# Layer norms of an encoder layer: where the low parts and the scaling by weight and bias run

## What is computed

```python
def _layer_norm(x, g, b, eps=LN_EPS):
    xf = x.astype(jnp.float32)
    mu = jnp.mean(xf, axis=-1, keepdims=True)
    var = jnp.mean(jnp.square(xf - mu), axis=-1, keepdims=True)
    return ((xf - mu) * lax.rsqrt(var + eps) * g + b).astype(x.dtype)

def layer(x, mem, l):
    x = _layer_norm(alpha * x + 0.5 * _swiglu(x, ...), ln_ffn1_g[l], ln_ffn1_b[l])
    x = _layer_norm(alpha * x + _token_mix(x, ...), ln_mix_g[l], ln_mix_b[l])
    x = _layer_norm(alpha * x + _memory_attn(x, mem, ...), ln_ca_g[l], ln_ca_b[l])
    return _layer_norm(alpha * x + 0.5 * _swiglu(x, ...), ln_ffn2_g[l], ln_ffn2_b[l])
```

## Time and profile before

| | us |
|---|---|
| median of 3 runs (4231.08 to 4235.39) | 4232.55 |
| the profiled execution, its own time | 4234.5 |
| its span in the trace | 4232.7 |
| PE busy in the span | 3664.0 (87%) |
| DVE / ACT / POOL busy | 1863.8 / 941.1 / 281.4 |
| POOL low parts (L564), 12 in ln1 to ln3, each 4.5 | 54.1 |
| stretch of ln1 (969.7 to 1037.8) | 68.1 |
| stretch of memln (2453.4 to 2489.9) | 36.5 |
| stretch of ln4 (4175 to the end) | 57.7 |

### The profile page before, as it was taken

How to read it: one execution, slowest core, us unless ns; L and a number is a source line. 1 busy time by engine, 2 the same in 40 slices (tenths; PEclk the granted TensorE clock), 3 DMA queues, 4 the chain that set the end, 5 groups by cost and what they waited for, 6 DMA issues and landing times. The chain is left out here.

```text
span 4232.7 us, 70217 instructions
## 1 busy us (share of the span) xinstructions
PE 3664.0 (87%) x29336; PEld 3110.1 (73%) x29336; DVE 1863.8 (44%) x2658; ACT 941.1 (22%) x1335; POOL 281.4 (7%) x361
## 2 busy tenths in 40 slices
PE   7999999996999545569889868977897999999997
PEld 6888888885888444248888656866785888888885
DVE  4444444446000375755444442331316454544446
ACT  2111111103111345432322332122303111111112
POOL 0000000001000052011222110010001000000000
PEclk9999999998999777779999979988998999999999
DMA  2101010101222202642122123001001010101001
GB/s 105 45 30 45 30 45 30 45 5 71 89 80 87 100 1 89 193 147 73 73 73 73 72 72 127 20 30 40 25 30 36 34 45 30 45 30 45 30 20 50
DMA packets 70899, 244.12 MB, mean 58 GB/s; under 512 B 5056, under 2 KB 30912, under 8 KB 64320
## 3 DMA queue, kind: packets, MB, share of 16 engines
q1 hardware_dynamic: 64528, 219.59, 14.6%
q10 hardware_dynamic: 6192, 21.89, 1.3%
HBM read 185.41 MB, written 56.05 MB: 57 GB/s over the span
## 5 line engine op out<-in xcount | busy, mean ns | idle before, releaser
L292 DVE TENSOR_TENSOR main_acc<-main_acc,ffn_psum 128x512 f32<-128x512 f32 (+1 forms) x1056 | 617.3, 598 | 854.2 <-PE ffn_psum L215 853.5
L204 PE MATMUL ffn_psum<-x_xh,ffn_wi_h 128*128 128x512 f32 (+1 forms) x2112 | 525.4, 357 | 52.5 <-DVE ffn_wi_l L281 52.5
L204 PE MATMUL ffn_psum<-x_xl,ffn_wi_h 128*128 128x512 f32 (+1 forms) x2112 | 525.5, 357 | 0.0
L204 PE MATMUL ffn_psum<-x_xh,ffn_wi_l 128*128 128x512 f32 (+1 forms) x2112 | 525.3, 357 | 0.0
L204 PEld LDWEIGHTS ffn_psum<-x_xh,ffn_wi_h 128*128 128x128 f32 x2112 | 372.7, 188 | 120.5 <-DVE ffn_wi_l L281 52.9
L204 PEld LDWEIGHTS ffn_psum<-x_xh,ffn_wi_l 128*128 128x128 f32 x2112 | 350.1, 188 | 60.7
L204 PEld LDWEIGHTS ffn_psum<-x_xl,ffn_wi_h 128*128 128x128 f32 x2112 | 349.7, 188 | 61.2
L215 PE MATMUL ffn_psum<-ffn_hid_h,ffn_wo_h 128*128 128x512 f32 (+1 forms) x1056 | 380.8, 361 | 12.6 <-DVE ffn_hid_l L300 10.0
L215 PE MATMUL ffn_psum<-ffn_hid_h,ffn_wo_l 128*128 128x512 f32 (+1 forms) x1056 | 377.6, 358 | 0.0
L215 PE MATMUL ffn_psum<-ffn_hid_l,ffn_wo_h 128*128 128x512 f32 (+1 forms) x1056 | 376.6, 357 | 0.0
L256 ACT CAST ffn_hid_h<-ffn_hid 128x1280 fp32r<-128x1280 f32 x44 | 55.6, 1265 | 1090.4 <-DVE ffn_hid L298 1090.4
(11 more groups left out here) (310 smaller groups left out, 5838.7 us busy)
## 6 DMA issues: line engine op xcount, KB each, us to landing
ffn_w_raw_in<-ffn_w_in_dram SPq DMA_DIRECT2D x44, 1024.0 KB, 5.3
rws_pack<-pack SPq DMA_DIRECT2D x40, 900.0 KB, 6.2
ffn_w_raw_out<-ffn_w_out_dram SPq DMA_DIRECT2D x44, 512.0 KB, 3.5
proj<-mixin_stage ACTq DMA_DIRECT2D x27, 640.0 KB, 3.0
mixin_w_raw<-mix_w_in_dram SPq DMA_DIRECT2D x27, 512.0 KB, 3.5
pack<-rwp_pack SPq DMA_DIRECT2D x4, 2580.0 KB, 10.5
rwp_raw<-proj SPq DMA_DIRECT2D x15, 640.0 KB, 8.4
kv_w_raw<-ca_w_kv_dram SPq DMA_DIRECT2D x16, 512.0 KB, 3.5
```

Source lines behind the costliest of these rows:

```text
L204: mm = nc.tensor.matmul(ps[:, at + c * BANK:at + c * BANK + tn], w[:, slot, cols], x[:, k, t0:t0 + tn], start=(k == 0 and j == 0), stop=(k ...
L292: nc.vector.tensor_tensor(acc[:, o, t0:t0 + tn], acc[:, o, t0:t0 + tn], ps[:, at:at + tn], ALU.add).then_inc(added, 1)
```

## The change

In every norm all eight tiles are scaled on ACT, and DVE scales none. The low part of every step is taken by DVE, after the normalising of the step that follows; POOL has no work in the norms. ACT's high part waits for one semaphore (`affine`) in place of two, and so does SP's store in ln4. The waiting of ACT for the constant `eps` stands at another place of the same list, before the same first instruction.

```diff
--- before.py
+++ after.py
@@ -450,9 +450,8 @@
         eps = m.sb("eps", [P, 1])
         ps = m.psum()
         mean_done, centred, squared, var_done = m.sem("mean_done"), m.sem("centred"), m.sem("squared"), m.sem("var_done")
-        rooted, rstd_done, scaled, affine_a, affine_v = m.sem("rooted"), m.sem("rstd_done"), m.sem("scaled"), m.sem("affine_a"), m.sem("affine_v")
-        high, low, const_set, stored = m.sem("high"), m.sem("low"), m.sem("const_set"), m.sem("stored")
-        HALF = KT // 2
+        const_set, rooted, rstd_done, scaled, affine = m.sem("const_set"), m.sem("rooted"), m.sem("rstd_done"), m.sem("scaled"), m.sem("affine")
+        high, low, stored = m.sem("high"), m.sem("low"), m.sem("stored")
         block = ctx.enter_context(nc.Block())
 
         def tok(s):
@@ -486,7 +485,6 @@
 
         @block.vector
         def _(dve):
-
             nc.vector.memset(eps[:], LN_EPS / scale ** 2).then_inc(const_set, 1)
 
             def centre(s):
@@ -501,15 +499,10 @@
                 dve.wait_ge(squared, s + 1)
                 nc.vector.tensor_tensor(acc[:, :, tok(s)], acc[:, :, tok(s)],
                                         rstd[:, s % 2, :].unsqueeze(1).broadcast_to([P, KT, NT]), ALU.mult).then_inc(scaled, 1)
-                dve.wait_ge(scaled, s + 1)
-                for k in range(HALF, KT):
-                    nc.vector.tensor_scalar(acc[:, k, tok(s)], acc[:, k, tok(s)], vecs[:, gain + k:gain + k + 1],
-                                            vecs[:, bias + k:bias + k + 1], ALU.mult, ALU.add).then_inc(affine_v, 1)
 
             def finish(s):
                 dve.wait_ge(high, s + 1)
-                if s == steps - 1:
-                    nc.vector.tensor_tensor(xl[:, :, tok(s)], acc[:, :, tok(s)], xh[:, :, tok(s)], ALU.subtract).then_inc(low, 1)
+                nc.vector.tensor_tensor(xl[:, :, tok(s)], acc[:, :, tok(s)], xh[:, :, tok(s)], ALU.subtract).then_inc(low, 1)
                 if after != 1.0:
                     dve.wait_ge(low, s + 1)
                     nc.vector.tensor_scalar(acc[:, :, tok(s)], acc[:, :, tok(s)], after, None, ALU.mult)
@@ -526,14 +519,13 @@
 
         @block.scalar
         def _(act):
-            act.wait_ge(const_set, 1)
-
             def square(s):
                 act.wait_ge(centred, s + 1)
                 if s >= 2:
                     act.wait_ge(var_done, s - 1)
                 nc.scalar.activation(squares[:, s % 2], acc[:, :, tok(s)], ACT.Square).then_inc(squared, 1)
 
+            act.wait_ge(const_set, 1)
             square(0)
             for s in range(steps):
                 act.wait_ge(var_done, s + 1)
@@ -543,32 +535,21 @@
                 if s + 1 < steps:
                     square(s + 1)
                 act.wait_ge(scaled, s + 1)
-                for k in range(HALF):
+                for k in range(KT):
                     nc.scalar.activation(acc[:, k, tok(s)], acc[:, k, tok(s)], ACT.Identity,
                                          bias=vecs[:, bias + k:bias + k + 1],
-                                         scale=vecs[:, gain + k:gain + k + 1]).then_inc(affine_a, 1)
+                                         scale=vecs[:, gain + k:gain + k + 1]).then_inc(affine, 1)
                 if out_d is None:
-                    act.wait_ge(affine_v, HALF * (s + 1))
-                    act.wait_ge(affine_a, HALF * (s + 1))
+                    act.wait_ge(affine, KT * (s + 1))
                     nc.scalar.copy(xh[:, :, tok(s)], acc[:, :, tok(s)]).then_inc(high, 1)
 
-        if out_d is None:
-            @block.sync
-            def _(sp):
+        @block.sync
+        def _(sp):
+            if out_d is None:
                 weights.start(sp)
-
-            @block.gpsimd
-            def _(pool):
-                for s in range(steps - 1):
-                    pool.wait_ge(high, s + 1)
-                    nc.gpsimd.tensor_tensor(xl[:, :, tok(s)], acc[:, :, tok(s)], xh[:, :, tok(s)],
-                                            ALU.subtract).then_inc(low, 1)
-        else:
-            @block.sync
-            def _(sp):
+            else:
                 for s in range(steps):
-                    sp.wait_ge(affine_a, HALF * (s + 1))
-                    sp.wait_ge(affine_v, HALF * (s + 1))
+                    sp.wait_ge(affine, KT * (s + 1))
                     sp.dma_start(out_d[:, :, tok(s)], acc[:, :, tok(s)]).then_inc(stored, 16)
                 sp.wait_ge(stored, 16 * steps)
```

## The result

| | before | after |
|---|---|---|
| median of 20 runs (lowest to highest), us | 4233.4 (4229.98 to 4241.03) | 4241.16 (4235.89 to 4248.87) |
| ratio, 95% interval | | 1.0018 (1.0011 to 1.0024) |
| span of the profiled execution | 4232.7 | 4239.6 |
| ln1: first root to end of its last instruction | 54.41 | 54.87 |
| memln, the same | 21.89 | 23.40 |

The change makes the kernel 7.8 us slower, 0.18%; forecast was 10.2 slower, 4242.8, in a range of 4239 to 4247. From their first roots on the five norms are 8.6 longer in the two traces (0.46 + 1.51 + 0.48 + 0.54 + 5.59).

The account below looks back on a forecast made before the run. The five norms were taken as bound by the chain inside each step, through ACT, with DVE limiting ln4's middle steps. +4.3 us for four norms and +5.9 for ln4 made +10.2 on 4232.55: 4242.8, range 4239 to 4247.

Parts of the forecast that it names:

- Root to scaling 4.62: In a norm step without POOL's disturbance, the time from ACT's root to the start of scaling: 4.62 us.
- the pitch of 0.493: Start-to-start spacing of ACT's scalings, 0.493 us, so four more add 1.97 in each of 22 steps.
- the 2.25 that POOL had put on the path: POOL's low part holds up DVE's normalising, some 2.25 us in each of 13 steps; the change removes it.
- the low part at 2.29 or less: Low part moved to DVE behind the next step's normalising: takes 2.29 us and costs nothing.
- the cover on DVE in ln3: In ln3 DVE finishes low part, factor and centring before ACT wants the centring, half a microsecond to spare.
- the step of 8.57 in ln4: In ln4 ACT's scaling becomes the limit: 4.62 to the scaling plus 3.95 to the next root, 8.57 us.
- Rival B: Norms: normalising is long for another reason than POOL's reading, so the stall stays, 29.3 us more, 4272; chance 0.03.
- rival A: Norms: scaling is cheaper on ACT without DVE scaling beside it, pitch 0.37, 11.4 us faster, 4221; chance 0.03.
- Rival C: DVE's cover fails in ln3, and PE's sums may slow in ln4: +1 to +4 us, 4244 to 4247; chance 0.09.
- I take nothing for it: Semaphores, one wait in place of two and one fewer to clear: counted as no change in time.
- I take 0.2: ln4: PE's last sum of squares slowed after idle time, between 0 and 0.3 us, taken as 0.2.
- 35.18 from first root to last scaling: Length of ln4 in the kernel before, 35.18 us, set against 38.90 forecast with the change.

Follow-up runs that it names:

- low_only: Kernel before with only the low parts moved to DVE, scaling still four on ACT and four on DVE; 4214.45 against 4234.43 us, ratio 0.9944.
- scaling_only: Kernel before with only the scaling moved, all eight on ACT, POOL keeping the low parts; 4270.82 against 4234.43 us, ratio 1.0079.
- the two kernels with two waits: The change with its scalings counted on two semaphores, in either order of the two waits; 4236.24 and 4243.39 us, one profiled execution each, on different chips.
- root_ahead: The change with ACT taking the next root and squares before this step's high part; 4223.27 against 4236.49 us for the kernel before, ratio 0.997.
- before_again: The kernel before, unchanged, profiled a second time; ln4 38.90 us in place of 37.25, first root to end of the last scaling.
- ln4_split: The change with ln4's scaling as before, four on ACT and four on DVE; one profiled execution, ln4 38.78 us against 42.84 in the change.
- two_waits: The change with the eight scalings counted on two semaphores, four on each, both waited for; 4236.24 us in one profiled execution.
- balanced: root_ahead with scalings divided between ACT and DVE step by step to suit DVE's load; 4204.55 against 4236.49 us for the kernel before, ratio 0.9925.

## Why the prediction came out as it did

**What held.** The direction, the mechanism and the size to within 2.4 us. Root to scaling 4.62, the pitch of 0.493, the 2.25 that POOL had put on the path, the low part at 2.29 or less, the cover on DVE in ln3 and the step of 8.57 in ln4 (measured 8.55) are all in the rows. Rival B fell in the kernel after and in low_only, rival A in the kernel after and in scaling_only. Rival C did not occur: ACT never waits for a centring in ln3, and in ln4 of the kernel after PE's sums stayed off the path.

**What was mis-sized.** Three terms, all of them small, and all to the same side:

- "I take nothing for it", for the semaphores. It was 0.06 to 0.07 in each of 17 steps with a high part, and some 0.07 more between the last high part and the last low part in ln1, ln2 and memln (2.00 before, 1.93 after). The steps are 10.49, not 10.56, and the sum of the four norms +3.0, not +4.3. The place of the 0.06 is shown by the two kernels with two waits. The other 0.07 has no run of its own, but in the ten traces these three norms have 2.00 where DVE has the semaphore instruction of its own and 1.93 or 1.94 where it has none.
- "I take 0.2" for PE's last sum in ln4. It cost nothing, since the sum took 5.41 in that trace, and ln4 came to +5.59 in place of +5.9. The reason given for the 0.2, the longer idle time, did not hold: after 4.82 of it the sum took 5.41, after 3.68 it had taken 6.53, and in root_ahead 6.77 after 4.82. Part of the 5.9 was also a step of 8.57 that is 8.55.
- ln4 before, 35.18 from first root to last scaling, was taken as what ln4 costs. It is what it cost in one execution. before_again, low_only and ln4_split show 1.5 to 1.7 more at the same place. By them the change costs some 7.0 in the norms, by the first trace 8.6, and the 7.8 between the medians lies between the two. How often each occurs in unprofiled runs was not measured. The interval of the ratio is 4.7 to 10.2 us and can't tell 7.0 from 8.6, nor 8.6 from the forecast, so that the median is near them is no proof of the single terms; the rows are.

**The chances.** 0.75 was put on slower by over 0.2% and 0.22 on within. The median came to 0.18%, with an interval of 0.11% to 0.24%: just within, on the less likely side, and the interval reaches past the line. The forecast had stood only 1.7 us beyond the line of 8.5. The first two terms above take 1.6 off it (8.6 by the traces, still at the line); what brought the median to 7.8, a longer ln4 in the kernel before or scatter, was not told apart. Stretches outside the norms differ by up to 1.4 us between the two traces with nothing changed in them, and the one from ln1 to memln lasts 1413 to 1425 over the ten traces. The first root of ln1 comes 11.81 after the phase's start in the traces of the kernel before and 13.50 in that of the change, but 11.81 in two_waits, whose ln1 is the same up to there. So that is scatter and no effect of the change.

## What to carry to other kernels

When an edit bundles two moves, price each by itself and run each by itself: here one half was worth 20 us, the other cost 36, and the bundle hid both. An engine that is off the critical path can still hold it up through another engine, as POOL's low part did with DVE's normalising. With ACT's order as it was, the low parts belonged on DVE and its four scalings had no reason to leave it: the slowest step of ln1 is 9.80 in low_only and 10.49 in the change. With the root taken early that turns for the middle steps, where DVE's load of some 9.8 would be longer than the 8.56 of eight scalings on ACT; balanced divides them so. low_only with the root taken early was not run. And before moving work between engines, look at what is merely queued on the path: the root that waited behind a high part for no reason of data cost 1.9 a step.

## What the hardware showed that was not expected

A wait for two semaphores costs 0.06 us more on ACT if the one that is met last is in an instruction of its own ahead of the one that waits; if that one is met early, it costs nothing (gaps of 0.09 and 0.03, in 17 places of each kernel); on DVE it goes with 0.07 (2.00 and 1.93). And sixteen matmuls of 128 x 256 after the same 3.88 us of idle time on PE took 5.12, 6.65, 6.75 and 6.77 in four executions (before, ln4_split, low_only, before_again) with the same instructions in ln4, at granted clocks of 0.72, 0.55, 0.54 and 0.54: a single trace is no fixed price for work at the edge of a clock change.
